# Linear attention in a two-layer hybrid decoder: output products grouped by kind, half-array products alternating between the two halves

## What is computed

```python
q_dec = qc * jnp.exp(cum)
k_inv = kc * jnp.exp(-cum)
scores = jnp.where(causal, jnp.einsum('bhnid,bhnjd->bhnij', q_dec, k_inv), 0.0)
o_intra = jnp.einsum('bhnij,bhnjv->bhniv', scores, vc)
...
_, prev = lax.scan(step, init, (jnp.moveaxis(total, 2, 0), jnp.moveaxis(kv_chunk, 2, 0)))
prev = jnp.moveaxis(prev, 0, 2)
o = o_intra + jnp.einsum('bhncd,bhndv->bhncv', q_dec, prev)
```

## Time and profile before

| | |
|---|---|
| median of 3 runs | 1114.74 us (1114.72 to 1115.62) |
| span of the profiled execution, first to last instruction | 1112.6 us; what lies around it isn't listed, and the median is 2.1 us above it |
| PE busy | 1093.3 us (98%) |
| DVE, ACT busy | 570.8 us (51%), 469.9 us (42%) |
| DMA | 313.15 MB, mean 281 GB/s; 425 to 430 GB/s in the middle of the experts' stretches |
| chain of waits, by engine | PE 87%, DMA 6%, DVE 4%, ACT 2% |

### The profile page before, as it was taken

The page is one execution under the profiler, slowest core; times in us unless marked ns, Lnnn a source line. Parts: engine busy times, 40 slices in busy tenths (PEclk is TensorE's granted clock), DMA queues, the critical chain, the costliest instruction groups (busy, mean ns, idle before and its releaser), DMA issues.

```text
span 1112.6 us, 14487 instructions
## 1 busy us (share of the span) xinstructions
PE 1093.3 (98%) x5868; PEld 758.4 (68%) x5868; DVE 570.8 (51%) x911; ACT 469.9 (42%) x758; POOL 2.6 (0%) x5
## 2 busy tenths in 40 slices
PE   8999999999999999999999999999999999999998
PEld 6998888888886344434479988888888753434433
DVE  6669574556665123223277686745575542323222
ACT  6677565566533001001266855755655421010101
POOL 0000000000000000000000000000000000000000
PEclk9999999999999999999999999999999999999999
DMA  9545454253777999999974344452439789999996
GB/s 377 223 152 190 148 189 155 76 227 151 277 293 312 428 430 425 430 426 427 422 275 183 130 187 151 152 181 88 186 151 355 258 357 429 429 426 427 428 427 280
DMA packets 24243, 313.15 MB, mean 281 GB/s; under 512 B 3184, under 2 KB 3312, under 8 KB 5744
## 3 DMA queue, kind: packets, MB, share of 16 engines
q1 hardware_dynamic: 23904, 312.22, 69.8%
q10 hardware_dynamic: 272, 0.00, 0.0%
HBM read 311.16 MB, written 1.05 MB: 281 GB/s over the span
## 4 chain that ended last, share of the span: by engine, by line
PE 87%; DMA 6%; DVE 4%; ACT 2%; issue 1%; DVEq 0%; SPq 0%; ACTq 0%
PE slot L665 35%; PE M L1014 16%; PE slot L1046 9%; PE slot L648 8%; DMA arena<-in_w_up 6%; PE slot L891 3%; PE slot L956 2%; PE slot L594 2%; PE M L849 1%; PE M L827 1%; PE slot L969 1%; PE M L969 1%; PE M L798 1%; PE M L838 1%; PE M L772 1%
## 5 line engine op out<-in xcount | busy, mean ns | idle before, releaser
L1473 DVE TENSOR_TENSOR w_lo<-ring,w_hi 128x1024 fp32r<-128x1024 f32 x198 | 238.1, 1222 | 153.2 <-ACT w_hi L1107 151.7
L1107 ACT ACTIVATE w_hi<-ring 128x1024 fp32r<-128x1024 f32 x200 | 207.8, 1054 | 99.3 <-PE slot L665 70.8
L665 PE MATMUL slot<-w_hi,hT_hi 128*128 128x512 f32 x480 | 192.5, 401 | 0.0
L665 PE MATMUL slot<-w_lo,hT_hi 128*128 128x512 f32 x480 | 187.3, 390 | 0.0
L665 PE MATMUL slot<-w_hi,hT_lo 128*128 128x512 f32 x480 | 187.0, 390 | 0.0
L1909 DVE TENSOR_TENSOR arena<-arena,M 128x512 f32<-128x512 f32 x16 | 11.0, 687 | 201.5 <-PE M L1014 201.5
L665 PEld LDWEIGHTS slot<-w_lo,hT_hi 128*128 128x128 f32 x480 | 90.1, 188 | 19.3
L665 PEld LDWEIGHTS slot<-w_hi,hT_hi 128*128 128x128 f32 x480 | 90.2, 188 | 18.8 <-issue 0.8
L665 PEld LDWEIGHTS slot<-w_hi,hT_lo 128*128 128x128 f32 x480 | 90.3, 188 | 18.1 <-issue 0.5
L648 PE MATMUL slot<-hT_hi,w_hi 128*128 128x256 f32 x256 | 73.4, 287 | 0.0
L648 PE MATMUL slot<-hT_hi,w_lo 128*128 128x256 f32 x256 | 72.4, 283 | 0.0
(11 more groups left out here) (302 smaller groups left out, 1667.3 us busy)
## 6 DMA issues: line engine op xcount, KB each, us to landing
ring<-in_w_mix SPq DMA_DIRECT2D x48, 2048.0 KB, 7.8
ring<-in_w_down SPq DMA_DIRECT2D x18, 2048.0 KB, 19.5
arena<-in_w_gate SPq DMA_DIRECT2D x12, 2048.0 KB, 19.1
ring_down<-in_w_gate SPq DMA_DIRECT2D x12, 2048.0 KB, 20.1
ring<-in_w_up SPq DMA_DIRECT2D x10, 2048.0 KB, 19.9
ring_up<-in_w_up SPq DMA_DIRECT2D x6, 2048.0 KB, 16.6
ring_odd<-in_w_up SPq DMA_DIRECT2D x6, 2048.0 KB, 20.8
arena<-in_w_up SPq DMA_DIRECT2D x6, 2048.0 KB, 22.2
```

Source lines behind the costliest of these rows:

```text
L665: last = mm(o[:, t * 512:(t + 1) * 512], h[:, 2 * n + cc, t * P:(t + 1) * P], w[:, cc * 512:(cc + 1) * 512], start=n == cc == k == 0, stop ...
L1107: A(piece_of(w_hi, i), source(i), ACT.Copy).then_inc(hi_ready.sem, 1)
L1473: v.tensor_tensor(piece_of(w_lo, i), source(i), piece_of(w_hi, i), ALU.subtract)\
```

## The change

The scores are formed with `hh` as the innermost loop, so that consecutive products lie on different halves of the array's rows. The outputs are formed in one place, after piece 1 of `J_Q + 2`: first the eight products of values and masked scores, then the wait for the state, then the twelve products of the state, with `hh` innermost. Only the first product in each bank of `M1` carries the start flag. The number and shapes of the products stay the same.

```diff
-                for hh in range(2):
-                    for g in range(2):
-                        for t in range(NT):
+                for g in range(2):
+                    for t in range(NT):
+                        for hh in range(2):
...
                 def gla_out(n):
 
-                    if n == 0:
+                    if n != 1:
                         return
-                    if n == 1:
-                        pe.wait_ge(gsc_sb.sem, gsc_sb.at(l, 1))
-                        pe.wait_ge(state_ready.sem, state_ready.at(l, 1))
-                    units = [(hh, g, t) for hh in range(2) for g in range(2) for t in range(NT)]
-                    for hh, g, t in units[3 * n - 3:3 * n]:
-                        o = M1[:, (hh * 4 + g * 2 + t) * P:(hh * 4 + g * 2 + t + 1) * P]
-                        hd = 2 * g + hh
-                        last = mm(o, va[:, t * 512 + hd * DV:t * 512 + (hd + 1) * DV],
-                                  gsc[:, (hh * 4 + g * 2 + t) * P:(hh * 4 + g * 2 + t + 1) * P],
-                                  start=True, stop=False, skip_group_check=True)
-                        for c2 in range(2 * t, 2 * t + 2):
-                            if c2:
+                    pe.wait_ge(gsc_sb.sem, gsc_sb.at(l, 1))
+                    for hh in range(2):
+                        for g in range(2):
+                            for t in range(NT):
+                                hd = 2 * g + hh
+                                block = slice((hh * 4 + g * 2 + t) * P, (hh * 4 + g * 2 + t + 1) * P)
+                                mm(M1[:, block], va[:, t * 512 + hd * DV:t * 512 + (hd + 1) * DV], gsc[:, block],
+                                   start=g == t == 0, stop=False, skip_group_check=True)
+                    pe.wait_ge(state_ready.sem, state_ready.at(l, 1))
+                    for g in range(2):
+                        for c2 in range(1, T // CH):
+                            for hh in range(2):
                                 last = mm(M1[:, (hh * 4 + g * 2) * P + c2 * CH:(hh * 4 + g * 2) * P + (c2 + 1) * CH],
                                           state[hh * DK:(hh + 1) * DK, (g * 3 + c2 - 1) * DV:(g * 3 + c2) * DV],
                                           q_dec[hh * DK:(hh + 1) * DK, g * T + c2 * CH:g * T + (c2 + 1) * CH],
-                                          start=False, stop=c2 == 2 * t + 1, skip_group_check=True)
-                    if n == PIECES - 1:
-                        last.then_inc(go_ps.sem, 1)
+                                          start=False, stop=g == 1 and c2 == T // CH - 1, skip_group_check=True)
+                    last.then_inc(go_ps.sem, 1)
```

## The result

Four runs each: 1105.94 us with the change (1105.81 to 1107.53) against 1115.1 before (1114.72 to 1115.62). The ratio is 0.9921, 95% interval 0.991 to 0.9933: faster by 0.8%. The profiled span fell from 1112.6 to 1103.9 us, by 8.7.

What follows compares the result with a forecast made beforehand. PE's own product stream was taken to bound the mixer. (3.73 outputs + 0.56 scores) x 2 layers = 8.58 us, taken off the median 1114.74: 1106.2 us; own range 1105.0 to 1107.5, up to 1110.0 for 8 times in 10.

Steps and rivals of the forecast that it cites:

- What bounds: In the mixer, only the length of PE's own stream of products sets the time; the experts follow PE.
- The outputs: Attention outputs in one insert: V 1.79, S 1.46, return 0.22, sum 3.47 against 7.20; 3.73 us saved per layer.
- state halves side by side and not in turns: The 24 state passes on alternating row halves cost as much as 12: 1.46 us, not 2.78.
- The scores: Score products alternating between halves start together, about 1.14 us against 1.71 for sixteen passes; 0.56 us saved per layer.
- S halves take turns: Rival, 9%: state products adding into PSUM don't overlap between halves; 5.9 us saved, so 1108.8, or 1110.6 without score overlap.
- Every change of half drains the array: Rival, 3%: each interleaved pass costs 0.20 us as a change; 1.2 us lost per layer, 1117.1, slower.
- Swallowed by the experts' weights: Rival, 8%: the experts' weight stream doesn't start earlier and gives all back, 1114.7; in one layer alone 1110.4.
- the weights' preparation: DVE's low parts for the job at 133.43: 4.6 us early, PE comes 3.73 earlier, 0.9 left; costed at nothing.
- The 2x: Skill rule, contraction of at most 64 rows: scores 0.82, S products 1.39, about 0.66 us more saved; forecast took less.
- The 62 ns per matmul: Skill rule on the sequencer: 24 state passes at least 1.49 us, saving smaller by 0.1 us or less; doubted.

Runs made afterwards that it cites:

- The runs with one ingredient each: Against the kernel before: only the scores alternate, 1113.9 us against 1114.9; only the outputs grouped with alternating state products, 1107.79 against 1114.9.
- the third run: As the change, but state products half by half, six then six, and scores in the old order; 1109.77 us against 1114.9 before.

## Why the prediction was right

- **What bounds.** PE alone in the mixer: the span fell by 8.7 us where the two mixers got shorter by 4.32 and 4.30. The runs with one ingredient each moved the stretch by just what their pieces say.
- **The outputs.** Forecast 1.79 + 1.46 + 0.22 = 3.47 us per layer, measured 1.78 + 1.49 + 0.19 = 3.46. The step that I chose between far bounds, state halves side by side and not in turns, was decided by rows of other products; the third run measured what order alone does to it. The change also drops most of the start flags; that moved nothing, since two value passes took 0.22 with them and 1.78 / 16 = 0.11 is the step without.
- **The scores.** Forecast 0.56 us per layer, measured 0.55.
- **The rivals.** "S halves take turns" would have shown 2.78 us, and 1.49 was measured, though these products add to PSUM. "Every change of half drains the array" would have cost 0.20 per pass; the scores take 1.09 us for sixteen. "Swallowed by the experts' weights" falls with the first issue, which moved by 4.46 us.
- **What hides the rest.** I had costed the weights' preparation at nothing, with at least 0.9 us left and some 2 more if ACT's chain moved too. The timeline of DVE shows the first low parts of the job at 128.97 begun at 124.95:

```profile
124.95 3.49 DVE L1472 TENSOR_TENSOR w_lo<-ring,w_hi 128x1024 fp32r<-128x1024 f32 x3
```

At some 1.2 us for one, the first is there at about 126.2, 2.8 us before PE needs it; before, it was 4.6. So 1.8 us of that cover are used up, and a further saving of this kind would have 2.8 left at this place.

- **The two rules of the Trainium skill.** The 2x (TensorEngine Tiling (Array Packing), Theoretical Speedup) would have made 0.82 us of the scores; the trace has 1.09, a factor of 1.5, since the old order overlapped in part already. The 62 ns per matmul (TensorE: Matmul & The Clock Gate, section "Wait — 56ns, not 53.3ns?") did not bind here: in the change, the state passes behind the first two of each half take (1.49 - 0.36) / 20 = 0.056 us each, and L753 runs at 0.045.
- **The number.** 1106.2 was forecast and 1105.94 measured, although the sum is 8.58 and the medians differ by 9.2. The excess over the span's 8.7 lies in the scatter of the runs (1114.72 to 1115.62 before, 1105.81 to 1107.53 after). So what was right is the 8.6 us; that the time itself came out within 0.3 us is luck.

Fewer changes of kind than one in and one out cannot be had while the state products stand between two projection pieces. Whether another place for them is cheaper wasn't tried.

## What to carry to other kernels

Where an engine's own stream is the bound, price a small product by its place: here, a change between full-array and half-array products costs 0.14 to 0.23 us, more than the pass of 0.11 us itself. The return to the projection points to the part of the array as what counts: it costs 0.19 to 0.23 behind the state products and 0.21 behind L753 (5.66 us for 24 passes instead of 5.45), but behind L848, whose fp32 products use the whole array, 12 passes take 2.75 us, within 0.03 of the plain length.

```profile
225.02 1.34 PE M L848 x12
226.36 2.75 PE slot L665 x12
```

Group products by the part of the array that they use, and within a group let consecutive products lie on different halves: of the outputs' 3.76 us per layer, grouping in one place without alternation gave 2.82, and alternation without grouping gave nothing. Take the steps from the chain's pieces, since durations of pipelined matmuls overlap and would give another sum.

## What the runs showed of the hardware that I had not expected

PE starts passes on an idle half of the array ahead of passes of the other half that stand before them in the program. In each of the three orders tried that have more than three passes of one half in a row, it did so when three of them were still to come. The start times of the single matmuls in the traces show it. They don't name the half, but the first pass on a half is recorded as longer (373 ns in the scores where later ones have 272, 320 in the state products), and from there on two rows of starts interleave, each in steps of 0.11 us. In the old scores this first pass of the second half starts at 88.759 us, 0.006 behind the fifth of the first half's eight. With six state products in a row it starts at 111.024, 0.006 behind the ninth pass of twelve, and in the runs of three at 109.698, 0.006 behind the third of six. The second layer has the same places.

The cost follows without a remainder: the second half is late by the time from the first pass to that one, which is 0.55 us in the scores, 0.94 and 0.27 in the two others, and 1.64 - 1.09, 2.43 - 1.49 and 1.76 - 1.49 are these very numbers. So, contrary to what I wrote of all engines at the start, PE does not keep its list's order between the two halves. What sets the reach of three wasn't tried.
